# Modulation sums placed between an attention head's last slabs, and out of the other mixers

## The reference

```python
branches = jnp.stack([o_a, o_b, o_c, o_d], axis=2)
gates = jax.nn.sigmoid(gate_logits.reshape(bsz, T, N_BRANCH, D_MODEL))
merged = jnp.sum(jnp.einsum('btnw,nwd->btnd', branches, w_branch[l]) * gates, axis=2)
h = h + _rms_norm(merged @ w_out[l], norm_mix_post[l])
f = _conv_ffn(_rms_norm(h, norm_ffn_pre[l]), ffn_w_up[l], ffn_conv_w[l], ffn_conv_b[l], ffn_w_down[l])
h = h + _rms_norm(f, norm_ffn_post[l])
```

```python
cond = jax.nn.silu(c)
for i in range(DEPTH):
    mod = (cond @ ada_w[i] + ada_b[i]).reshape(bn, N_SUBLAYERS, 3, D_MODEL)
```

## Time and profile before

| | |
|---|---|
| three executions | 2538.77, 2540.63, 2552.21 us; median 2540.63 |
| the profiled execution | 2553.17 us; its span 2551.4 us |
| mean granted TensorE clock | 0.944 of 2.4 GHz |
| busy share of the span | PE 92%, PEld 84%, DVE 57%, ACT 42%, POOL 31% |
| DMA | 429.27 MB, mean 168 GB/s |
| loads of modulation tiles | 144, 512 KB each |

### The profile page before, as it was taken

The page is one execution under the profiler, slowest core; times in us unless marked ns, Lnnn a source line. Parts: engine busy times, 40 slices in busy tenths (PEclk is TensorE's granted clock), DMA queues, the critical chain, the costliest instruction groups (busy, mean ns, idle before and its releaser), DMA issues.

```text
span 2551.4 us, 41098 instructions
## 1 busy us (share of the span) xinstructions
PE 2347.3 (92%) x16612; PEld 2149.0 (84%) x16612; DVE 1457.9 (57%) x2443; ACT 1061.8 (42%) x1930; POOL 800.2 (31%) x769
## 2 busy tenths in 40 slices
PE   6889889989998888989989989998899999988998
PEld 6677659879997677569889979987899999878998
DVE  4664556559847666466489654449544444435443
ACT  4444232245545443222455444432444444445443
POOL 2441002126624341012146434315243243221431
PEclk9998789989998998789989989999899999999999
DMA  6663237636674663247546745653356555533554
GB/s 211 169 174 105 96 103 263 231 99 215 217 237 125 184 176 105 89 154 266 195 144 223 243 137 183 183 155 132 118 188 182 158 184 183 170 121 119 187 180 126
DMA packets 121949, 429.27 MB, mean 168 GB/s; under 512 B 14960, under 2 KB 16928, under 8 KB 121633
## 3 DMA queue, kind: packets, MB, share of 16 engines
q1 hardware_dynamic: 94208, 333.80, 40.0%
q0 software_dynamic: 27408, 91.77, 12.5%
q10 hardware_dynamic: 144, 1.07, 0.1%
HBM read 425.48 MB, written 1.10 MB: 167 GB/s over the span
## 4 chain that ended last, share of the span: by engine, by line
PE 76%; DVE 12%; DMA 4%; POOL 4%; ACT 3%; issue 2%; DVEq 0%; ACTq 0%; POOLq 0%
PE bank L357 20%; PE bank L359 20%; PE bank L358 20%; PE bank L680 4%; DMA ada_ring<-in_ada 4%; PE bank L386 3%; DVE s_sb L1379 2%; POOL ring_lo L1987 2%; DVE std L1413 2%; PE bank L417 1%; DVE ring_lo L1391 1%; DVE s_sb L1418 1%; PE bank L347 1%; PE bank L508 1%; PE bank L550 1%
## 5 line engine op out<-in xcount | busy, mean ns | idle before, releaser
L357 PE MATMUL bank<-x_hi,ring_hi 128*128 128x256 f32 (+2 forms) x3552 | 1045.7, 294 | 70.7 <-DVE x_lo L1379 21.2
L358 PE MATMUL bank<-x_lo,ring_hi 128*128 128x256 f32 (+2 forms) x3552 | 1029.1, 290 | 0.0
L359 PE MATMUL bank<-x_hi,ring_lo 128*128 128x256 f32 (+2 forms) x3552 | 1026.1, 289 | 0.0
L1391 DVE TENSOR_TENSOR ring_lo<-ring,ring_hi 128x1024 fp32r<-128x1024 f32 (+1 forms) x437 | 593.7, 1359 | 609.7 <-ACT ring_hi L814 609.6
L357 PEld LDWEIGHTS bank<-x_hi,ring_hi 128*128 128x128 f32 x3552 | 688.6, 194 | 98.8 <-issue 21.2
L814 ACT ACTIVATE ring_hi<-ring 128x1024 fp32r<-128x1024 f32 (+1 forms) x551 | 570.2, 1035 | 376.6 <-PE bank L359 271.1
L359 PEld LDWEIGHTS bank<-x_hi,ring_lo 128*128 128x128 f32 x3552 | 690.3, 194 | 0.0
L358 PEld LDWEIGHTS bank<-x_lo,ring_hi 128*128 128x128 f32 x3552 | 688.6, 194 | 0.7
L1987 POOL TENSOR_TENSOR ring_lo<-ring,ring_hi 128x1024 fp32r<-128x1024 f32 (+1 forms) x155 | 373.0, 2407 | 816.4 <-ACT ring_hi L814 505.7
L359 PE MATMUL bank<-hid_hi,ring_lo 128*128 128x256 f32 (+1 forms) x1056 | 299.3, 283 | 0.0
L357 PE MATMUL bank<-hid_hi,ring_hi 128*128 128x256 f32 (+1 forms) x1056 | 298.1, 282 | 0.0
(11 more groups left out here) (275 smaller groups left out, 2290.4 us busy)
## 6 DMA issues: line engine op xcount, KB each, us to landing
ring<-in_w_gu SPq DMA_DIRECT2D x192, 512.0 KB, 3.5
ada_ring<-in_ada POOLq DMA_DIRECT2D x144, 512.0 KB, 5.2
ring<-in_w_in SPq DMA_DIRECT2D x136, 512.0 KB, 4.1
ring<-in_ffn_up SPq DMA_DIRECT2D x104, 512.0 KB, 3.5
ring<-in_w_down SPq DMA_DIRECT2D x64, 512.0 KB, 3.5
ring<-in_w_branch SPq DMA_DIRECT2D x32, 512.0 KB, 3.6
ring<-in_ffn_down SPq DMA_DIRECT2D x32, 512.0 KB, 4.1
ring<-in_w_down SPq DMA_DIRECT2D x32, 384.0 KB, 3.3
```

The source lines that it names most:

```text
L357: pe.matmul(b[:, cs], ring_hi[:, i_hi, c0], x1, start=first and k == 0, stop=False)
L358: pe.matmul(b[:, cs], ring_hi[:, i_hi, c0], x2, start=False, stop=False)
L359: m = pe.matmul(b[:, cs], ring_lo[:, i, c0], x1, start=False, stop=last and k == nk - 1)
L1391: dve.tensor_tensor(ring_lo[:, i, 0:cols], ring[:, i, 0:cols], ring_hi[:, n % HIGH, 0:cols].bitcast(f32), ALU.subtract).then_inc(split(n)[ ...
```

## The change

Only the places of the calls, their numbers and POOL's rule for loading are changed. POOL's `ada(n)` now issues n loads at once. In the heads DVE's `ada(2)` moves up, ahead of the last one or two slabs of the half-head; POOL's calls in the heads stay in their places. The calls at a layer's start and in GLA go, MLA's have 1 instead of 2 and stand between `scores_c` and `weights_c`, a turn of the merge has 3 (the first two turns) or 4, and the first three columns of the down products have 2.

```diff
-        ADA = {"lat": 3, "head": 2, "gla": 3, "mla": 2, "merge": 3}
+        ADA = {"head": 2, "mla": 1, "merge": 4}
...
 DVE
                 for _ in range(n):
                     t = tiles_done[0]
+                    if t == len(ada_order):
+                        return
...
             def mixers(l):
                 latents(l)
-                ada(ADA["lat"])
                 low_halves("aq", l, 0)
...
                 low_halves("dq", l, 0)
+                ada(ADA["head"])
                 low_halves("dv", l, 0)
-                ada(ADA["head"])
                 scores_d(l, 0)
                 low_halves("aq", l, 1)
                 weights_d(l, 0)
                 low_halves("ak", l, 1)
+                ada(ADA["head"])
                 low_halves("av", l, 1)
                 out_d(l, 0)
-                ada(ADA["head"])
                 scores_a(l, 1)
                 low_halves("dq", l, 1)
                 weights_a(l, 1)
+                ada(ADA["head"])
                 out_gate(l, 0, 0)
                 out_gate(l, 0, 1)
-                ada(ADA["head"])
                 scores_d(l, 1)
...
                 low_halves(*gate_of(l, 0, 3))
-                ada(ADA["gla"])
                 masked(l, 1)
                 low_halves(*gate_of(l, 1, 0))
                 states(l, 1)
                 rope_q(l, 0)
-                ada(1)
                 finish_a(l, 2)
                 for hd in range(4):
                     scores_c(l, hd)
                     if hd < 3:
                         low_halves(*gate_of(l, 1, 1 + hd))
+                    ada(ADA["mla"])
                     weights_c(l, hd)
...
                         finish_b(l, hd - 2, 1)
-                    ada(ADA["mla"])
...
             def merge(l):
...
                     if j < 2:
-                        ada(2)
+                        ada(3)
...
             def ffn(l):
...
                         low_halves("down", l, j, part)
-                    ada(1)
+                    ada(2 if j < 3 else 1)
...
 POOL
-            loads, owed = [0], [0]
+            loads = [0]
...
             def ada(n):
 
-                load_ada(owed[0])
-                owed[0] = n
+                load_ada(n)
...
                     load_ada(ADA_RING)
-                ada(ADA["lat"])
...
                 low_halves(*gate_of(l, 0, 3))
-                ada(ADA["gla"])
                 low_halves(*gate_of(l, 1, 0))
-                ada(1)
```

## The result

The changed kernel takes 2510.61 us (median of 4 runs, 2507.32 to 2516.40); the kernel before, on the same chip, 2543.48 us (2538.77 to 2552.21). These medians are 32.9 us apart. The ratio on record is 0.9855, 95% interval 0.9826 to 0.9883, that is 1.5%, some 37 us, faster; a recorded ratio is not the quotient of the two medians, which here would be 0.9871. A second comparison on another occasion gave 0.9837 (0.9823 to 0.9850).

A forecast was written before the change was run, and what follows sets the result against it. TensorE, 92% busy, was held by VectorE's waits for modulation tiles to land; 22.2 + 3.6 + 7.8 + 8.6 - 2.0 = 40.2 us off 2553.2 profiled gives 2513.0, against the median 2500.4, forecast 2500; range 2480 to 2526.

The forecast's parts named there:

- Heads, stalls 22.2 us: Attention heads: TensorE's idle time behind scores, queries and copies of V goes, 22.2 us; bounds 0 and 23.4.
- TensorE's clock, 8.6 us: Stretches behind removed stalls, in heads and GLA: TensorE regains work lost below 2.4 GHz, 8.6 us; bounds 0 and 8.6 + 14.5.
- the rival that had the clock give more: Layer 0's long stretch at 0.56 goes whole, or half of each layer's: 14.5 us more, 2486; chance 0.13.
- Start of a layer, 3.6 us: Three sums removed there: layer 0's wait for k_a shrinks by 3.6 us, layer 1 gains 0; bounds 0 and 6.4.
- GLA, 7.8 us: Second GLA pair: waits for masks behind sums shrink by 4.2 us in layer 0, 3.6 in layer 1; bounds 0 and 10.8.
- MLA and down products, 0: Moved or added sums fit VectorE's waits there, cost 0; worst 9.6 us in MLA, 6 x 1.2 = 7 in down products.
- Merge, -2.0 us: Added sums delay the merge's start by 1.0 us a layer and fit later turns; bounds 0 and 19 us lost.
- The rival that needed 2.6 us a turn: Merge: an added sum meeting POOL's low half costs 1.2 + 2.2 us a turn, 54 us in all, 2553; chance 0.03.
- Contention: Layer 1's heads: sums meeting POOL's low halves might take 2.2 us each, 15.4 us longer on DVE; priced at 0.

## Why the prediction came out

The sign, the size and the range were right. The working was for the profiled execution: 40.2 us off, and it is 42.3. Part of that closeness is luck. TensorE's idle time fell by 28.3 us where the working had 31.6, and its busy time by 14.0 where it had 8.6; the two errors nearly cancel. And the wait that it removed was the right one, but not for the reason it gave first, the new places. Against the medians it said 2500 of 2540.6, 1.6%; measured 1.5%. The forecast is 10.6 us low, because the profile of the kernel before lay 12.5 us above the median that the forecast started from, and the changed kernel's only 0.3 above its own; the larger gain took 2.1 us of this back. Point by point:

- *Heads, stalls 22.2 us.* Measured 19.7 of TensorE's idle time. What the working has wrong is its cause: it describes the new place and the new loading at once, and never asks what each is worth. The answer was in the earlier trace rows: from 81.39, two sums behind the high copy end near 84.4 and the scores begin at 86.95, so with the tile there the old place costs nothing. The experiments give 0.9862 for the rule alone and 0.9834 for the change without the places. That POOL's loads come at the same time but are read one call later, and that 5 us are long enough, held: no sum in the heads of the changed kernel waits for a landing. (The slab behind the sums is later by 2.3 us, from 82.06 to 84.4, and not by the 2.9 of the working; nothing depends on it.) TensorE's waits for V's transposes behind scores are 0.6 and 1.8 us, 2.4 in all, a little over the forecast of under 2; the 1.8 is in layer 1's first scores (0.3 before), which stand on VectorE behind a multiply that took 2.61 us beside a low half of GpSimd. It is there with the loading rule alone too, and it is 0.2 us in the new heads alone and with two sums at the merge's start, so it does not follow the places.
- *TensorE's clock, 8.6 us.* Undersized: the heads alone gave 12.8 us of busy time against my 6.2. I had left out the stretch behind k_a's wait (0.50 for 5.35 us from 69.95 on, 2.7 us) and what is spread over shorter ones in layer 1. In GLA of layer 0, 3.3 us of busy time went; in layer 1's 1.4 us came. The long stretch at 0.56 did not go: in layer 0 24 us of it (260 to 284) ran at 0.50. So the rival that had the clock give more was wrong about the place, though the clock did give 5.4 us more than the working had.
- *Start of a layer, 3.6 us.* The wait for k_a is 2.83 us, forecast 2.8; the stage is 4.9 us shorter, 3.5 of it idle time. In layer 1 it went from 1.99 to 1.88, forecast 0.
- *GLA, 7.8 us.* The waits for the masks are gone in layer 0 and 3.20 us in layer 1, forecast 0 and 3. In layer 0 the next wait took 0.96 us of it: TensorE's wait for the state is 3.71 us and was 2.75. Idle time fell by 6.6 us in all.
- *MLA and down products, 0.* MLA is 0.2 us shorter and 0.01 longer.
- *Merge, -2.0 us.* Measured -0.95 and -2.2, for the reason given (the sums ahead of the first low halves), and undersized in layer 1, where three sums ended 1.6 us too late, and a load of GpSimd that waited for a late sum held its low half 1.2 us. The rival that needed 2.6 us a turn is ruled out: past the third turn TensorE is busy throughout. But what it feared exists one stage on: in the gated products a second sum costs 1.5 us a pair, more than half of it through GpSimd's queue.
- *Contention.* I kept 0 with 15.4 us as the other end, from the multiply of the earlier trace rows. Zero is right for the time, but in the heads the sums are not what was lengthened. In layer 1's heads thirteen of sixteen sums ran beside a low half of GpSimd and none took over 1.208 us. GpSimd's low halves yielded. First the changed kernel, then the one with no sums in the heads:

```profile
L1986 POOL TENSOR_TENSOR ring_lo<-ring,ring_hi x9: 2494/4462/5554, 783.9 to 906.3; 128x1024 fp32r<-128x1024 f32 x9
```
```profile
L1978 POOL TENSOR_TENSOR ring_lo<-ring,ring_hi x9: 2387/2397/2679, 804.5 to 926.9; 128x1024 fp32r<-128x1024 f32 x9
```

(minimum, median, maximum in ns.) A median of 4.46 us instead of 2.40, up to 5.55, cost nothing that shows, for the heads last as long without any sums (131.07 and 131.06 us); TensorE takes those slabs three slabs later. The Trainium skill, GPSIMD Engine Reference, Key points, says that the two engines share the SBUF interfaces with contention for two-input instructions of VectorE; by that rule I had let the sums be longer. That there is contention the trace confirms, and a sum can be the one that is lengthened: in the kernel before one took 2.76 us (from 120.04 on) beside a low half of GpSimd that had begun first, at 119.37:

```profile
120.04 2.76 DVE L1408 CUSTOM_DVE_ANT_0 ada_ring<-ada_ring,cond 128x1024 f32<-128x1024 f32 x1
```

Which of the two is lengthened is taken up at the end.

## To carry to other kernels

Before an operation is moved out of the way, ask whether it is in the way or only waits there: two lines that issued each load one call earlier gave 31 of the 32.5 us that the heads gained, and a total that can't be told from that of the new order and distribution. A free place is free for a number of operations and for nothing else: two or three sums of 1.15 us fit between the slabs, and one late tile there cost more than it had in the old place. And when sums are spread over idle stretches of one engine, look at what each one makes another engine issue: in the gated products more than half of the price was GpSimd's, for where its issues stood in its queue.

## What I had not expected of the hardware

- VectorE and GpSimd on one SBUF access seem to take turns, not to share. VectorE's sums beside a low half of GpSimd kept 1.20 to 1.21 us, while that low half took up to 5.55 us instead of 2.40; a low half of VectorE beside one of GpSimd took 3.40 us in one place and 1.21, as long as alone, in another (from 798.57 on). One line of each kind, from the changed kernel:

```profile
797.03 4.96 POOL L1986 TENSOR_TENSOR ring_lo<-ring,ring_hi 128x1024 fp32r<-128x1024 f32 x1
```
```profile
875.20 3.40 DVE L1391 TENSOR_TENSOR ring_lo<-ring,ring_hi 128x1024 fp32r<-128x1024 f32 x1
```

  In the first, VectorE did two sums and a low half without a gap until 799.78, and GpSimd ended 2.2 us after that; five more of GpSimd's low halves in layer 1's heads ended 2.2 to 2.3 us after such a row of VectorE's. In the second, GpSimd was at work from 874.35 to 877.52, and VectorE ended 1.1 us after it. Mostly the one that came later paid. What lets a row of VectorE's go through while GpSimd waits, and why the low half at 875.20 did not go through behind its sums, is open; no run here varies it.
- Equal work and an equal wait don't fix the clock. With a k_a wait of 2.8 us the first heads ran at 1.00 and lasted 130.28 us in the changed kernel; with the same wait they ran at 0.98 and lasted 132.22 us in the kernel with two sums at the merge's start, whose program is the same up to there: TensorE was granted 0.50 for the 4.4 us behind that wait, and 1.00 in the changed kernel. Layer 1's MLA lasted 81.2 us at 0.82 with the loading rule alone, and 88.3 us at 0.75 with the new heads alone, though the two differ only inside the heads; 6.1 of these 7.1 us are busy time. Some 6 us between two kernels of this study can be that alone.
